# The one-token shift of the first stage: SBUF-to-SBUF DMA and a VectorE subtraction in place of fp32 products

## The chip, the cores and the metric

The kernel runs on one core of a Trainium2 chip. The metric is the time of one execution on the device in microseconds (us); lower is better. A kernel before and a kernel after are compared by the ratio of their medians over repeated runs.

## What is computed

The reference is two transformer-like layers over 256 tokens of width 2048, all in fp32: a block with an RWKV-7 mixer, an mLSTM mixer and a mixture of experts, then two attention layers. The change touches only the start of the RWKV mixer:

```python
u = x @ w_in[i]                                   # (1, 256, IN_COLS)
u_r, u_m, u_g = _split(u, [RWKV_COLS, MLSTM_COLS, GATE_COLS])   # RWKV_COLS = 3360
...
z_prev = jnp.pad(z, ((0, 0), (1, 0), (0, 0)))[:, :-1]
z = z + mu * (z_prev - z)                         # z is u_r
r, k, v, zw, za, zg = _split(z, [1024, 1024, 1024, 64, 64, 160])
```

Each token's row gets `mu` times the difference between the row of the token before and its own. The first token has zeros before it.

## The kernel before

Tokens lie on partitions: token 128 b + p is on partition p, in half b of a tile. So `UR`, the tile of `u_r`, is 128 partitions x 2 halves x 3360 columns, and the token before is on the partition before; only the first token of the second half has its predecessor on partition 127 of the first half.

The products are made with fp32 values split in two float32r halves each (`hi` and `lo`), three products for one. The weight columns come in blocks of 512 (six of them, and a seventh of 288), and a block's weights in eight pieces of 256 rows (512 KB, in the seventh 288 KB). Each piece goes through a chain: SyncE issues its load into one of six buffers as soon as the piece that was there has been halved; ScalarE writes the high half (`split_to` on ScalarE), VectorE the low half (`split_to` on VectorE, L283); TensorE runs 12 matmuls on it. There are three buffers for the halves, so the high half of a piece waits until TensorE has used the piece three before it. Pieces are counted from 0 over the whole kernel; block ci has the pieces 8ci to 8ci + 7. `ahead_of(key)` halves the pieces up to two beyond the one with which `key`'s sum ends, `more(1)` one more, and each engine works its instructions off in the order in which they are written.

For each block `ci` TensorE runs the projection (`proj_a`, L1282), takes a PSUM buffer for `ur.shift` (L1283), waits for `ur.copied` (L1285), which is ScalarE's copy of the block out of PSUM into `UR` (`out_of`, L2713), and multiplies with `shiftd` (ones on the superdiagonal minus the identity) and `carry` (one element that brings partition 127 of the first half into partition 0 of the second), L1286 to L1288. VectorE waits for this sum and for `mub` (mu on all partitions), multiplies it in PSUM and adds it to `UR` (L2251, L2252). Its event `("ur", ci)` is what the RWKV stage waits for. PSUM is a ring of four buffers; a `take` gets the one that was taken longest ago and waits until it was freed. `shiftd` and `carry` are built by Pool (GpSimd) at the start (L2806 to L2810).

Behind the seventh block the RWKV stage begins: TensorE runs three pieces of another projection (`ml.qk`, whose low halves Pool makes), transposes the gates (`rw.lo`, after ScalarE's tanh and sigmoid on the seventh block, L2379 to L2381), then two more pieces and the lora products, which need `loraT`; VectorE multiplies the keys, squares and sums them (L1403 to L1406) before it copies `loraT` (L1411 to L1416).

Of the kernel before, what the change touches and what calls it, by code (L numbers as in the profile page):

```python
# [9 lines left out]
ALU = mybir.AluOpType  # L10
# [328 lines left out]
def build(nc, I, out, plan=None, last=False):  # L339
    with ExitStack() as ctx:  # L340
# [7 lines left out]
        def at(o, n, dt=F32):  # L348
            names[0] += 1
            assert o + n <= TOT, o + n  # L350
            return nc.alloc_sbuf_tensor_at(f"t{names[0]}", [128, n], dt, offset=base + 4 * o)[:, :]

        def alloc(n, dt=F32):
            o = top[0]
            top[0] = o + n + -n % 8
            return at(o, n, dt)

        def tm(c):
            return alloc(2 * c).rearrange("p (b c) -> p b c", b=2)
# [7 lines left out]
        def bufs(nraw, nhalf):  # L367
# [9 lines left out]
        ident, shiftd, carry, ucent, tri_inc, tri_str = [alloc(128) for _ in range(6)]  # L377
# [15 lines left out]
        UR = tm(3360)  # L393
# [4 lines left out]
        PB, QB, RB, BB = tm(1024), tm(1024), tm(1024), tm(1024)  # L398
# [16 lines left out]
        kstate = alloc(8 * 64).rearrange("p (i v) -> p i v", i=8)  # L415
        pz = alloc(8)
        mub = at(fmbase, 3360)
        par = [RB.rearrange("p b c -> p (b c)")[:, 0:1024], RB.rearrange("p b c -> p (b c)")[:, 1024:2048],
               at(lt_at + 1280, 1024)]
        r_, k_, v_ = [UR[:, :, 1024 * i:1024 * i + 1024] for i in range(3)]  # L420
# [142 lines left out]
        def two(v, n):  # L563
            return v.unsqueeze(1).broadcast_to([128, 2, n])

        def half(v):
            return v.rearrange("p (b n) -> p b n", b=2)
# [5 lines left out]
        def tensor_program(e):  # L573
            pe = Tensor(e, counts, ring, stream, ident)
# [71 lines left out]
            def proj_a(*args, **kw):  # L646
                for _ in pieces_a(*args, **kw):
                    pass
# [5 lines left out]
            def some(work, n):  # L654
                for _ in range(n):
                    next(work, None)
# [615 lines left out]
            first = pieces_a(pe, "ur0", xT, 16, "w_in", 0, 512)  # L1272
            for j, part in enumerate(((0,), (0, 1), (1, 2), (2, 3, 3))):
                turn_columns("in.xT", x, j, (f"landed.in{j}",), ("ident",))
                for i in part:
                    pe.wait_ge(("in.xTc", i))
                    some(first, 1)
            pe.wait_ge(("consts",))
            for ci, c in enumerate(range(0, 3360, 512)):
                n = min(512, 3360 - c)  # L1280
                if ci:
                    proj_a(pe, f"ur{ci}", xT, 16, "w_in", c, n)  # L1282
                v = half(pe.take("ur.shift", ci))[:, :, 0:n]  # L1283
                d = UR[:, :, 512 * ci:512 * ci + n]
                pe.wait_ge(("ur.copied", ci))  # L1285
                pe.mm(v[:, 0, :], shiftd, d[:, 0, :], True, True)  # L1286
                pe.mm(v[:, 1, :], shiftd, d[:, 1, :], True, False)
                pe.mm(v[:, 1, :], carry, d[:, 0, :], False, True, event=("ur.shift", ci))  # L1288
            pe.stage("rwkv")
            rwkv()  # L1290
            rows_of("ml.if", "w_if", xT, (0, 8), 8, "pool")
# [10 lines left out]
            v = pe.take("pl.T", of=(2,)).rearrange("p (k b t) -> p k b t", k=4, b=2)  # L1302
# [51 lines left out]
        def vector_program(e):  # L1354
            v = Vector(e, counts, ring, stream)
# [888 lines left out]
                v.split_to(2 * j + 2)  # L2244
            for ci, c in enumerate(range(0, 3360, 512)):
                n = min(512, 3360 - c)
                v.ahead_of("ur.shift", ci)
                ps = half(v.bank("ur.shift", ci))[:, :, 0:n]
                d = UR[:, :, 512 * ci:512 * ci + n]
                v.wait_ge(("ur.shift", ci), ("landed.mu",))  # L2250
                v.tt(ps, ps, two(mub[:, 512 * ci:512 * ci + n], n), ALU.mult)  # L2251
                v.tt(d, d, ps, ALU.add, event=("ur", ci))  # L2252
                v.free("ur.shift", ci)
            v.stage("rwkv")
            rwkv()
            gate_rows()
# [13 lines left out]
            for c in range(4):  # L2270
# [8 lines left out]
                     event=("mi.lo", c))  # L2279
# [46 lines left out]
            first = stream.first("w_in_odd_2")  # L2326
# [16 lines left out]
            for ci in range(4):  # L2343
                cs = slice(512 * ci, 512 * ci + 512)
                for b in range(2):
                    v.stt(hn[:, b, cs], x[:, b, cs], inv[:, b:b + 1], rwt[:, cs], ALU.mult, ALU.mult,
                          event=("out.h", ci) if b else None)


        def scalar_program(e):  # L2350
            a = Scalar(e, counts, ring, stream)
# [16 lines left out]
            def out_of(key, o, ci, f=ACT.Copy, scale=1.0, event=None, tokens=True):  # L2368

                a.ahead_of(key, ci)  # L2370
                ps = a.bank(key, ci)
                a.wait_ge((key, ci))
                ps = half(ps)[:, :, 0:o.shape[2]] if tokens else ps.rearrange("p (m t) -> p m t", m=4)
                a.activation(o, ps, f, scale=scale, event=event)
                a.free(key, ci)
# [335 lines left out]
            for ci, c in enumerate(range(0, 3360, 512)):  # L2711
                n = min(512, 3360 - c)
                out_of(f"ur{ci}", UR[:, :, c:c + n], 0, event=("ur.copied", ci))  # L2713
            a.stage("rwkv")
            rwkv()
            high_halves("rw.yT", yrT, 1024)
# [24 lines left out]
            first = stream.first("w_pg")  # L2741
# [23 lines left out]
            for j in range(4):  # L2765
                ps = a.bank("ev.T", j).rearrange("p (b k t) -> p b k t", b=2, k=4)
                a.wait_ge(("ev.T", j), j > 1 and ("r1.sum", j - 2) or None)
                a.activation(squares[j % 2].rearrange("p (k b t) -> p b k t", k=4, b=2), ps, ACT.Square,
                             event=("r1.square", j))
# [10 lines left out]
            first = stream.first("w_in_odd_2")  # L2780
# [18 lines left out]
        def pool_program(e):  # L2799
            g = Pool(e, counts, ring, stream)  # L2800
# [2 lines left out]
            g.memset(ones, 1.0)  # L2803
            g.memset(ident, 0.0)
            g.asel(ident, ident, ALU.not_equal, 1.0, 0, [[-1, 128]], 1, event=("ident",))
            g.memset(shiftd, 0.0)  # L2806
            g.asel(shiftd, shiftd, ALU.not_equal, 1.0, 1, [[-1, 128]], 1)
            g.asel(shiftd, shiftd, ALU.not_equal, -1.0, 0, [[-1, 128]], 1)
            g.memset(carry, 0.0)
            g.asel(carry, carry, ALU.not_equal, 1.0, -127, [[128, 128]], 1)  # L2810
            g.asel(tri_inc, one, ALU.is_ge, 0.0, 0, [[1, 128]], -1)
            g.asel(tri_str, one, ALU.is_gt, 0.0, 0, [[1, 128]], -1)
            g.memset(ucent, -CD)
# [4 lines left out]
            for l in range(6):  # L2818
                b = 1 << l
# [96 lines left out]
            for l in range(5):  # L2916
                n = 1 << l
# [6 lines left out]
            for l in range(3):  # L2924
                n = 1 << l
# [87 lines left out]
        with nc.Block() as block:  # L3013
            @block.sync
            def _(e):
                sync_program(e)

            @block.tensor
            def _(e):
                tensor_program(e)  # L3020

            @block.vector
            def _(e):
                vector_program(e)

            @block.scalar
            def _(e):
                scalar_program(e)

            @block.gpsimd  # L3030
            def _(e):
                pool_program(e)
# [55 lines left out]
```

## Time and profile before

| | us |
|---|---|
| median of three runs | 3218.98 |
| lowest and highest run | 3209.98, 3226.59 |
| span of the profiled execution | 3213.3 |
| TensorE busy in it | 3035.3 (94%) |
| VectorE, ScalarE, Pool busy in it | 1550.1, 837.7, 266.6 |
| the first stage in it, to the last shift product | 0 to about 190 |

The profile is one execution. PE is TensorE's matmuls, PEld its weight loads, DVE VectorE, ACT ScalarE, POOL GpSimd, SP SyncE; nearly every instruction is recorded in a helper of the program (L137 the matmul, L143 the transpose, L254 ScalarE's activation, L283 VectorE's two-operand operation), so shapes and moments tell them apart. L83 and L2970 are DMA issues. The time behind "<-" in brackets is for how long the engine had been idle, and what ended it. A granted clock (PEclk) of 1.00 is 2.4 GHz, 0.50 is 1.2 GHz.

### The profile page before, as it was taken

How to read it: one execution, taken by the hardware profiler on the slowest of the kernel's cores; microseconds unless marked ns; L12 is line 12 of the kernel's file. 1: busy time of each engine (PE TensorE's matmuls, PEld its weight loads, DVE VectorE, ACT ScalarE, POOL GpSimd, SP SyncE). 2: the span in 40 equal slices, each digit the busy share in tenths (PEclk: the TensorE clock that was granted, in tenths of full speed). 3: DMA queues.
4: the chain of work that ended last, by engine and by line, in shares of the span. 5: the costliest groups of instructions: out<-in, count | busy, mean ns of one | idle time of the engine just before them, and what ended most of it. 6: DMA issues, size and time to landing. Idle time of an engine off the chain costs nothing.

```text
span 3213.3 us, 42675 instructions
## 1 busy us (share of the span) xinstructions
PE 3035.3 (94%) x18308; PEld 2171.3 (68%) x18308; DVE 1550.1 (48%) x1862; ACT 837.7 (26%) x926; POOL 266.6 (8%) x245
## 2 busy tenths in 40 slices
PE   8999999899999999999999999799999999999998
PEld 6787777899987733333333333288768878997886
DVE  4465544674555513222222322438886554444655
ACT  3342222544433311011101100110001334443443
POOL 2042111000000000000000000054330000000000
PEclk9999988999998999999999999899999999999899
DMA  7543221456564599999999999743333465887443
GB/s 243 152 136 99 74 67 55 119 161 180 177 228 152 211 413 425 425 425 425 425 425 425 425 425 425 291 140 118 117 119 118 144 175 122 184 189 158 99 158 138
DMA packets 215216, 722.10 MB, mean 225 GB/s; under 512 B 16170, under 2 KB 18634, under 8 KB 164716
## 3 DMA queue, kind: packets, MB, share of 16 engines
q1 hardware_dynamic: 210716, 702.22, 62.6%
q0 software_dynamic: 3216, 14.97, 1.3%
q8 instruction: 146, 2.39, 0.3%
q10 hardware_dynamic: 1088, 2.10, 0.2%
q14 instruction: 50, 0.41, 0.0%
HBM read 717.13 MB, written 2.10 MB: 224 GB/s over the span
## 4 chain that ended last, share of the span: by engine, by line
PE 73%; DMA 12%; DVE 10%; ACT 4%; issue 1%; POOL 0%; DVEq 0%; ACTq 0%
PE psum L137 72%; DMA t<-in_w_up 11%; DVE t L283 7%; ACT t L254 2%; PE psum L143 1%; DVE t L294 1%; ACT t L256 1%; DVE t L298 0%; DVE t L306 0%; ACT L254 0%; POOL t L328 0%; DVE t L269 0%; ACT L256 0%; DMA t<-in_x 0%; DVE t L275 0%
## 5 line engine op out<-in xcount | busy, mean ns | idle before, releaser
L137 PE MATMUL psum<-t,t 128*128 128x256 f32 (+10 forms) x17230 | 2941.4, 380 | 125.5 <-DVE t L283 69.3
L137 PEld LDWEIGHTS psum<-t,t 128*128 128x128 f32 (+4 forms) x17230 | 2080.0, 175 | 948.1 <-issue 580.3
L283 DVE TENSOR_TENSOR t<-t,t 128x1024 fp32r<-128x1024 f32 (+6 forms) x642 | 785.0, 1223 | 502.1 <-ACT t L254 469.1
L254 ACT ACTIVATE t<-t 128x1024 fp32r<-128x1024 f32 (+8 forms) x521 | 528.5, 1014 | 924.5 <-PE psum L137 661.2
L283 DVE TENSOR_TENSOR t<-t,psum 128x1024 f32<-128x1024 f32 (+3 forms) x265 | 246.4, 930 | 739.5 <-PE psum L137 439.0
L254 ACT ACTIVATE t<-psum 128x1024 f32<-128x1024 f32 (+5 forms) x278 | 213.5, 768 | 1408.7 <-PE psum L137 1310.4
L328 POOL TENSOR_TENSOR t<-t,t 128x1024 f32<-128x1024 f32 (+9 forms) x125 | 209.0, 1672 | 545.4 <-DVE t L283 258.2
L283 DVE TENSOR_TENSOR t<-psum,t 128x1024 f32<-128x1024 f32 (+5 forms) x125 | 100.2, 802 | 131.6 <-PE psum L137 103.0
L143 PE MATMUL psum<-t,t 128*128 128x128 f32 (+1 forms) x566 | 87.7, 294 | 32.1 <-DVE t L294 18.4
L143 PEld LDWEIGHTS psum<-t,t 128*128 128x128 f32 (+1 forms) x566 | 67.3, 149 | 69.6 <-issue 39.8
L83 POOL DMA_DIRECT2D t<-in_s_lr x1 | 0.6, 574 | 1185.1 <-DVE t L306 1185.1
L269 DVE COPY t<-psum 128x256 f32<-128x256 f32 (+4 forms) x82 | 47.7, 582 | 105.8 <-PE psum L143 59.6
L294 DVE SCALAR_TENSOR_TENSOR t<-t,t,t 128x512 f32<-128x512 f32 (+4 forms) x80 | 49.4, 618 | 3.0
L254 ACT ACT_TABLE_LOAD x38 | 48.8, 1283 | 4.6 <-issue 1.4
L298 DVE TENSOR_REDUCE t<-t 128x4 f32<-128x512 f32 (+9 forms) x58 | 47.5, 819 | 3.5 <-ACT t L254 1.4
L302 DVE TENSOR_TENSOR_SCAN t<-t,t 128x256 f32<-128x256 f32 (+1 forms) x65 | 44.7, 688 | 2.2
L290 DVE TENSOR_SCALAR t<-t,t,t 128x64 f32<-128x64 f32 x128 | 40.2, 314 | 4.6
L137 PE MATMUL psum<-t 64*64 64x64 f32 (+2 forms) x512 | 36.2, 267 | 6.5 <-ACT t L254 5.8
L83 POOL DMA_DIRECT2D t<-in_final_norm_g x1 | 0.6, 567 | 483.4 <-PE psum L137 483.4
L137 PEld LDWEIGHTS psum<-t 64*64 64x64 f32 (+2 forms) x512 | 30.0, 172 | 10.0 <-ACT t L254 7.5
L269 DVE COPY t<-t 64x64 f32<-64x64 f32 x64 | 30.2, 472 | 2.2
L256 ACT ACTIVATE t<-psum,t 128x256 f32<-128x256 f32 (+1 forms) x56 | 24.9, 444 | 21.5 <-PE psum L137 15.1
(65 smaller groups left out, 237.9 us busy)
## 6 DMA issues: line engine op xcount, KB each, us to landing
t<-in_w_gate SPq DMA_DIRECT2D x128, 1024.0 KB, 16.9
t<-in_w_up SPq DMA_DIRECT2D x128, 1024.0 KB, 18.4
t<-in_w_down SPq DMA_DIRECT2D x128, 1024.0 KB, 17.4
t<-in_w_in SPq DMA_DIRECT2D x160, 512.0 KB, 4.3
t<-in_w_in_odd SPq DMA_DIRECT2D x128, 512.0 KB, 5.3
t<-in_w_in_even SPq DMA_DIRECT2D x96, 512.0 KB, 3.8
t<-in_w_out SPq DMA_DIRECT2D x32, 512.0 KB, 4.7
t<-in_w_pg SPq DMA_DIRECT2D x32, 512.0 KB, 4.1
```

What stands on the lines that cost most here:

```text
L83: self.e.dma_start(out, in_).then_inc(self.counts.sem(name), 16)
L137: ins = self.e.matmul(o, l, r, start=start, stop=stop, skip_group_check=True)
L143: ins = self.e.transpose(o, i, self.ident[0:k, 0:k])
L254: self.put(self.e.activation(o, i, f, scale=scale), event)
L256: self.put(self.e.activation(o, i, f, bias=bias, scale=scale), event)
L269: self.put(self.e.tensor_copy(o, i), event)
L283: self.put(self.e.tensor_tensor(o, a, b, op), event)
L290: self.put(self.e.tensor_scalar(o, a, s1, s2, o1, o2), event)
L294: self.put(self.e.scalar_tensor_tensor(out=o, in0=a, scalar=s, in1=b, op0=o1, op1=o2), event)
L298: self.put(self.e.tensor_reduce(o, i, AX.X, op), event)
L302: self.put(self.e.tensor_tensor_scan(o, d0, d1, init, o0, o1), event)
L328: self.put(self.e.tensor_tensor(o, a, b, op), event)
```

## The change

The products with `shiftd` and `carry` go, with their constants and their PSUM buffers. ScalarE, after it has copied a block into `UR`, waits for its own copy and, from block 2 on, for VectorE's addition of two blocks before, and issues two DMAs from its own queue: partitions 0 to 126 of the block to partitions 1 to 127 of `prior`, and the row of partition 127, first half, to partition 0, second half. `prior` is double-buffered, in the region of `QB`, which is used only later. Partition 0 of the first half is zeroed once by Pool. VectorE waits for both DMAs, subtracts (`prior` - `UR`) into `gap` (the region of `BB`), multiplies by mu and adds. Ahead of the wait it halves the pieces up to 8ci + 10 (`split_to(8 * ci + 11)` ends before piece 8ci + 11), and one more between the subtraction and the multiplication.

```diff
@@ names @@
+        prior = [QB.rearrange("p b c -> p (b c)")[:, 1024 * k:1024 * k + 1024].rearrange("p (b c) -> p b c", b=2)
+                 for k in range(2)]
+        gap = BB[:, :, 0:512]
@@ tensor_program @@
-            pe.wait_ge(("consts",))
             for ci, c in enumerate(range(0, 3360, 512)):
                 n = min(512, 3360 - c)
                 if ci:
                     proj_a(pe, f"ur{ci}", xT, 16, "w_in", c, n)
-                v = half(pe.take("ur.shift", ci))[:, :, 0:n]
-                d = UR[:, :, 512 * ci:512 * ci + n]
-                pe.wait_ge(("ur.copied", ci))
-                pe.mm(v[:, 0, :], shiftd, d[:, 0, :], True, True)
-                pe.mm(v[:, 1, :], shiftd, d[:, 1, :], True, False)
-                pe.mm(v[:, 1, :], carry, d[:, 0, :], False, True, event=("ur.shift", ci))
@@ vector_program @@
-                v.ahead_of("ur.shift", ci)
-                ps = half(v.bank("ur.shift", ci))[:, :, 0:n]
+                v.split_to(8 * ci + 11)
+                p_ = prior[ci % 2][:, :, 0:n]
                 d = UR[:, :, 512 * ci:512 * ci + n]
-                v.wait_ge(("ur.shift", ci), ("landed.mu",))
-                v.tt(ps, ps, two(mub[:, 512 * ci:512 * ci + n], n), ALU.mult)
-                v.tt(d, d, ps, ALU.add, event=("ur", ci))
-                v.free("ur.shift", ci)
+                v.wait_ge(("landed.prior", ci), ("landed.mu",))
+                v.tt(gap[:, :, 0:n], p_, d, ALU.subtract)
+                v.more(1)
+                v.tt(gap[:, :, 0:n], gap[:, :, 0:n], two(mub[:, 512 * ci:512 * ci + n], n), ALU.mult)
+                v.tt(d, d, gap[:, :, 0:n], ALU.add, event=("ur", ci))
@@ scalar_program @@
                 out_of(f"ur{ci}", UR[:, :, c:c + n], 0, event=("ur.copied", ci))
+                a.wait_ge(("ur.copied", ci), ("first.row",), ci > 1 and ("ur", ci - 2) or None)
+                p_ = prior[ci % 2][:, :, 0:n]
+                a.load(("landed.prior", ci), [(p_[1:128], UR[0:127, :, c:c + n]), (p_[0:1, 1:2], UR[127:128, 0:1, c:c + n])])
@@ pool_program @@
-            g.memset(shiftd, 0.0)
-            g.asel(shiftd, shiftd, ALU.not_equal, 1.0, 1, [[-1, 128]], 1)
-            g.asel(shiftd, shiftd, ALU.not_equal, -1.0, 0, [[-1, 128]], 1)
-            g.memset(carry, 0.0)
-            g.asel(carry, carry, ALU.not_equal, 1.0, -127, [[128, 128]], 1)
+            for k in range(2):
+                g.memset(prior[k][0:1, 0, :], 0.0, event=("first.row",))
```

## Rows read from the trace of the kernel before

**Rows 1.** Page, busy time, share of the span and instructions by engine.
```profile
PE 3035.3 (94%) x18308; PEld 2171.3 (68%) x18308; DVE 1550.1 (48%) x1862; ACT 837.7 (26%) x926; POOL 266.6 (8%) x245
```

**Rows 2.** Busy time in stretches: stretch, length, engines, clock, DMA share; shift 2 to 3.
```profile
66.19:92.46 26.27, 25.16 (x102) 19.15 (x102) 12.26 (x10) 9.50 (x9) 0.00 (x0) 1.00 0.55 160
```

**Rows 3.** Timeline of 65 to 80 us: start, duration, engine, operation; a full boundary.
```profile
65.12 1.02 ACT L254 ACTIVATE t<-psum 128x1024 f32<-128x1024 f32 x1 [1.70 <-PE psum L137]
...
66.19 14.00 PE L137 MATMUL psum<-t,t 128*128 128x512 f32 x54 [1.11 <-ACT t L254]
...
69.07 1.23 DVE L283 TENSOR_TENSOR psum<-psum,t 128x1024 f32<-128x1024 f32 x1 [4.40 <-PE psum L137]
70.34 1.22 DVE L283 TENSOR_TENSOR t<-t,psum 128x1024 f32<-128x1024 f32 x1
...
71.92 1.06 ACT L254 ACTIVATE t<-t 128x1024 fp32r<-128x1024 f32 x1 [4.63 <-PE psum L137]
...
77.49 1.06 ACT L254 ACTIVATE t<-t 128x1024 fp32r<-128x1024 f32 x1 [1.73 <-PE psum L137]
```

**Rows 4.** Chain of waits from 118 to 206 us: start, duration, what.
```profile
170.25 1.03 ACT t L254
...
171.33 2.86 PE psum L137 x6
...
177.62 9.88 PE psum L137 x72
...
187.52 0.66 ACT t L254
...
196.88 0.31 ACT t L254
...
199.03 1.06 PE psum L143 x8
200.09 6.13 PE psum L137 x49
```

**Rows 5.** DMA between 3204 and 3214 us, ScalarE's stores: packets, queue, issues.
```profile
DMA packets 1088, 2.10 MB, mean 210 GB/s; under 512 B 64, under 2 KB 64, under 8 KB 1088
...
q10 hardware_dynamic: 1088, 2.10, 54.0%
...
out<-t ACTq DMA_DIRECT2D x4, 512.0 KB, 2.7
```

**Rows 6.** DMA between 194 and 195.6 us, the load of the 65 rows of `w_w2`.
```profile
DMA packets 78, 0.27 MB, mean 166 GB/s; under 512 B 13, under 2 KB 13, under 8 KB 78
```

**Rows 7.** PE's wait in the timeline of 231 to 237 us, and clock by stretches.
```profile
236.03 1.23 PE L137 MATMUL psum<-t,t 128*128 128x256 f32 x8 [2.78 <-POOL t L328]
...
236.00:240.00 4.00, 3.98 (x23) 3.98 (x24) 3.93 (x3) 0.00 (x0) 3.86 (x1) 0.66 0.48 131
240.00:244.00 4.00, 4.00 (x36) 4.00 (x35) 3.97 (x2) 0.00 (x0) 2.70 (x2) 0.91 0.50 135
244.00:248.00 4.00, 4.00 (x23) 4.00 (x23) 3.93 (x3) 1.23 (x2) 2.42 (x1) 0.57 0.41 131
```

**Rows 8.** DMA between 162 and 166 us, loads of 1152-byte packets.
```profile
DMA packets 354, 0.39 MB, mean 97 GB/s; under 512 B 16, under 2 KB 354, under 8 KB 354
...
q1 hardware_dynamic: 354, 0.39, 40.8%
```

**Rows 9.** Timeline behind the last block and, last, at 231 us.
```profile
190.78 0.75 DVE L283 TENSOR_TENSOR t<-t,psum 128x576 f32<-128x576 f32 x1
...
191.64 3.54 DVE L283 TENSOR_TENSOR t<-t,t 128x2048 f32<-128x2048 f32 x1
...
195.21 4.37 DVE L283 TENSOR_TENSOR t<-t 128x2048 f32<-128x2048 f32 x1
...
203.95 0.48 DVE L279 MEMSET t<- 1x512 f32 x1 [0.16 <-DVE t L269]
...
231.37 2.29 DVE L283 TENSOR_TENSOR t<-t 128x2048 f32<-128x2048 f32 x1
```

**Rows 10.** DMA issues up to 240 us: size, median time to landing.
```profile
t<-in_w_in SPq DMA_DIRECT2D x64, 512.0 KB, 4.5
```

## What will the change do to the time?

> **What bounds the kernel now.** I read the page first: PE is busy 94% of a span of 3213.3 us [rows 1], so what PE waits for or works off counts directly. The change touches the first stage only, so I went on to the busy time by stretches, one stretch for each column block. The reader should see that a full block takes 26.3 us, of which PE is busy 25.2, while VectorE (12.3) and ScalarE (9.5) are half idle [rows 2]. The timeline of one boundary shows what the missing 1.1 us and part of the busy time are [rows 3]. I call T the moment when the last projection product of a block ends. ScalarE copies the block out of PSUM (65.12 to 66.14), PE waits 1.11 us for that, then does the shift (66.19 to 69.05, three fp32 products that appear as six matmuls), and VectorE multiplies by mu and adds (1.23 + 1.22 us). After this ScalarE's halvings of the next pieces start 2.79 us apart (71.92 to 77.49 for two): this is the time of one piece, 12 matmuls, and eight pieces are 22.4 us. So the shift costs PE 26.3 - 22.4 = 3.9 us for each full block. The chain of waits has the last two: 4 us from 170.23 to 174.19, then 0.7 us of waiting after 187.49 and six matmuls of 0.28, until VectorE multiplies at 189.98 and adds at 190.78 [rows 4, 9]. Between T = 170.23 and T = 187.49 lie 17.3 us, with the narrow block's eight pieces of 1.6 us (72 matmuls, six pieces, in 9.88).
>
> **What is removed and moved.** PE loses the wait and the products: six times 3.9 us, and 2.4 in the last block, at most 26 us. Not all of it is to be had. The PSUM ring takes the buffer used longest ago; without the shift's own buffers, block 1 falls on block 0's, so that boundary keeps the 1.2 us wait for the copy: 2.7 instead of 3.9. Pool's five constant builders go and two one-partition memsets come: Pool's instructions are done before the first T in any case, nothing. VectorE's two operations become three. The subtraction I price as the fp32 operation of the same size, 1.23 us (0.76 in the narrow block) [rows 3]. With the gaps: 1.27 a step.
>
> **What the new wait holds back.** VectorE now waits for the landing before it subtracts, and it is a queue in order: behind the wait stand the low halves of the next weight pieces, without which PE has nothing. Written out: before the wait VectorE has halved pieces up to the third of the next block (8ci+10); the fourth (8ci+11) comes after the subtraction, the fifth (8ci+12) only after mu and the addition. With L for the landing, counted from T: the fourth is ready at L + 2.6, the fifth at L + 6.4. PE wants the fifth at T + 4 x 2.8 = 11.2. So the landing is free up to L = 4.7, and each us above it costs a us at every full boundary. VectorE gets to the wait at about T + 4.5, because ScalarE now issues two DMAs ahead of the third piece's high half. There is no slack to speak of. The weight loads, too, are issued on SyncE as pieces are halved, and stand still with VectorE.
>
> **How long the transfer takes.** This decides the case. It is 127 partitions with 2 runs of 2048 bytes each, 254 packets. The nearest row in direction and queue is ScalarE's store at the end: 512 KB on 128 partitions, 2.7 us from issue to landing; its four stores left 1088 packets, 64 of them tiny, so 16 tiny ones (the completion of each DMA engine) for a DMA. The share of 54.0% of 16 engines over 10 us is 86.4 us, 84 ns for each of 1024 packets of 2 KB [rows 5]. On 16 engines the data are 16 x 84 ns = 1.34 us and the rest, 1.36 us, is fixed.
>
> But does a DMA of 127 partitions get 16 engines? The trace has one load whose partitions are not a multiple of 16, `w_w2` with 65 rows of 4 KB. In its stretch there are 78 packets, 13 of them tiny [rows 6]: 65 data packets and 13 completions, so 13 engines with 5 rows each, where 16 engines with uneven shares would have left 16. The hardware gave equal shares. That admits two rules: the largest number up to 16 that divides the count (65 = 13 x 5), or shares of the count over 16 rounded up (5, which just fills 13). For 127, a prime, the first gives one engine, the second 16. I take the first, because equal shares is what the row shows and for 127 only one engine gives them.
>
> The Trainium skill, page DMA: Bandwidth & Descriptors, section Why a DMA increments its semaphore by 16 and not by 1, says that a DMA from the SP or ACT queue uses the largest k up to 16 that divides the slowest dimension, and names 127 partitions as k = 1; the rounded-up shares it knows for the software queue. By that rule the transfer is the serial one, by the rounded-up rule the transfer of rival one; this trace's 13 completions for 65 rows agree with it and do not exclude the other.
>
> One engine: 254 x 84 ns = 21.3 us. The bounds are 1.34 us (16 engines) and twice 21.3 (if an engine that reads and writes SBUF takes twice the time of one that only does one of them; no row has that). I take 21.3, since loads and stores have the same packet time. Beside it the weight loads go through the same engine with 16 packets each, 1.34 us; two of them fall into the wait (the pieces whose halving frees a buffer just before T and at T + 4.5), then they stop with VectorE: 2.7 us, between 0 and 5.4. So L = 1.1 (copy and semaphore) + 1.36 + 21.3 + 2.7 = 26.5.
>
> **The sum.** A full boundary, blocks 0 to 4: 26.5 to the landing, 6.4 until the fifth piece can start, four more pieces 4 x 2.8 = 11.2, together 44.1. PE has then stood still for some 20 us. In this trace a wait of PE of 2.78 us, at 233.25 to 236.03, is followed by stretches with a granted clock of 0.66, 0.91 and 0.57, that is 2.7 + 0.7 + 3.4 = 6.9 us at the lower level of 1.2 GHz, 3.4 us of PE's work [rows 7]. Here the first us of such a loss fall into VectorE's time; I take 1.0 for a boundary, between 0 and 3.4. So 45.1 against 26.3: +18.8, five times: +94.
> Block 5's shift beside the narrow block: its loads are 288 KB, so L is 25.4; two steps of 1.27, the subtraction too, and two low halves of 0.8 make the fifth piece ready 5.4 later; four pieces of 1.6 are 6.4; clock 0.8. 38.0 against 17.3: +20.7.
> The last block: 254 packets of 1152 bytes. The narrow loads' row gives 40.8% of 16 engines over 4 us for 338 data packets, 77 ns, waits for HBM in it [rows 8]; by bytes it is 84 x 1152/2048 = 47. I take 51, nearer to the latter since the source is SBUF: 13.0 us. Landing at T + 0.75 + 1.36 + 13.0 + 4 (three loads of ml.qk) = 19.1, three steps of 0.8: the block is ready at T + 21.5, where it was ready at 191.53, T + 4.0 [rows 9]. Behind it VectorE's chain for the key norm runs 12.8 us (191.64 to 204.43 [rows 9]) to the lora inputs; 3.3 of them were Pool's doing (3.54 and 4.37 us where an operation of that size took 2.29 with Pool idle [rows 9]), and Pool will be idle. PE needs the gates (tanh at 196.88, transposes at 199.03: 2.2 later, so at T + 23.7), then the transposes and two pieces (1.1 and 6.0 us, and 1.5 for the clock) and the lora inputs (T + 31.0): the first lora product at T + 32, against 206.1, T + 18.6 [rows 4]: +13.4.
> Sum: 94 + 20.7 + 13.4 = +128 us. The later stages wait for this one's results and move with it; the stage of the experts is bound by loads that start only when the mixer is done. The profiled execution spans 3213.3 us, 5.7 under the median of 3219.0; on the median it gives 3347 us. The bounds together (no contention, no clock: -19 and -6; double contention and full clock loss: +19 and +16; packet time 10% up or down: +-14; an issue on ScalarE that lasts until the engine has taken the descriptors: +9) make 3295 to 3425 for this case.
>
> **Rival one, faster: the transfer is spread over 16 engines.** L is then 1.1 + 2.7 = 3.8 with nothing beside it, and 1.1 + 4.5 = 5.6 at the weight loads' median [rows 10]. Below 4.7 no stall: 4 x 3.9 + 2.7, and 0.6 for block 5 (there the three steps on VectorE eat the rest, as PE wants a piece every 1.6 us), nothing at the end: -19, 3200 us. At 5.6: 0.9 lost at six boundaries, 3205 us. For it: the row of 65 rows bears the rounded-up shares as well. It would turn into a loss from L = 8.
>
> **Rival two, much slower: one engine at half the rate between SBUF and SBUF.** 21.3 more at six boundaries and 13 at the last: +141 on the forecast, 3488 us. Against it: nothing in the trace shows an engine below 84 ns for 2 KB unless HBM kept it waiting.
>
> **How the numbers follow.** One engine at the packet time of the trace: 0.80, at 3347 us. Rival one 0.12, rival two 0.08; the range leaves these out, 2 in 10, and is that of the likeliest case. A measurement of this kernel can tell 0.5%, 16 us. The first rival lies on that bound, 14 to 19 us faster: 0.07 faster, 0.05 within. Slower: 0.88.
>
> **What the profile after would show.** For the forecast: on ScalarE's queue 254 data packets and one completion for a transfer, a landing some 25 us after the issue; VectorE idle on that DMA seven times, some 20 us each; PE standing after the third piece of each block, for VectorE; 45 us from block to block; a low granted clock just after. If ScalarE's DMA instruction itself lasts for 20 us, PE stands a piece earlier. Against it: 16 completions for a transfer and landings under 6 us. It would be wrong in size if packets in SBUF took another time than 84 ns.

## The result, and the profile after

| | before | after |
|---|---|---|
| median, us | 3215.69 (4 runs) | 3351.84 (4 runs) |
| ratio, 95% interval | | 1.0419 (1.0398 to 1.0440) |
| span of the profiled execution | 3213.3 | 3352.8 |

The kernel after is 4.2% slower, 136 us on the medians, against a forecast of 3347 us. The first rows are the chain of waits of the kernel after, 30 to 360 us (share by line, then start, duration, what), around one block boundary, then the last block. They answer to [rows 4].

```profile
by line: DMA t<-t 49.4%; PE psum L137 37.6%; DVE t L283 6.6%; ACT t L254 3.3%; ACTq L83 1.7%; PE psum L143 0.6%; issue 0.6%; ACT L254 0.4%; DVEq L77 0.1%; ACTq L77 0.0%
...
84.53 1.03 ACT t L254
85.59 0.75 ACTq L83
86.37 24.50 DMA t<-t
110.90 1.24 DVE t L283
112.26 1.24 DVE t L283
113.54 16.04 PE psum L137 x60
129.60 1.04 ACT t L254
...
304.51 0.66 ACT t L254
305.19 0.73 ACTq L83
305.96 16.76 DMA t<-t
322.74 2.76 DVE t L283
325.52 0.77 DVE t L283
326.32 0.77 DVE t L283
```

The reader should see one repeated pattern: copy (84.53), DMA of 24.5 us, two steps of VectorE (the subtraction and the low half of the fourth piece), then the last five pieces of the block on TensorE (60 matmuls), and the next copy at 129.60. T, the end of the block's last projection product, is 84.51, just before the copy; the landing (VectorE's start at 110.90) is 26.4 later, the period from copy to copy 45.07 us. In the kernel before the DMA has no place in that chain.

What the engines do in that time, from the timeline of 84 to 118 us, answers to [rows 3].

```profile
85.59 13.30 ACTq L83 DMA_DIRECT2D t<-t  x2
98.94 3.40 ACT L254 ACTIVATE t<-t 128x1024 fp32r<-128x1024 f32 x3 [13.38 <-issue]
...
101.31 5.49 PE L137 MATMUL psum<-t,t 128*128 128x512 f32 x12 [11.21 <-DVE t L283]
...
110.90 7.82 DVE L283 TENSOR_TENSOR t<-t,t 128x1024 f32<-128x1024 f32 x6 [9.64 <-DMA t<-t]
...
113.54 4.83 PE L137 MATMUL psum<-t,t 128*128 128x512 f32 x12 [6.74 <-DVE t L283]
```

TensorE stands 11.2 us, does one piece, stands another 6.7, and the pieces after a wait take 5.49 and 4.83 us where a piece in stride takes 2.8. The busy time by stretches tells why (the number behind the busy times of the five engines is the granted clock, 1.00, 0.50 and 0.50 here, which answers to [rows 7]):

```profile
88.00:92.00 4.00, 2.09 (x9) 1.33 (x8) 0.00 (x0) 0.00 (x0) 0.00 (x0) 1.00 0.07 21
...
96.00:100.00 4.00, 0.00 (x0) 0.00 (x0) 0.00 (x0) 1.06 (x1) 0.00 (x0) 0.50 0.07 26
100.00:104.00 4.00, 2.69 (x6) 2.16 (x7) 1.23 (x1) 2.11 (x2) 0.00 (x0) 0.50 0.43 137
```

And the transfer itself, from the DMA view of 85.5 to 111 us, which answers to [rows 5] and [rows 6]:

```profile
q10 hardware_dynamic: 287, 0.52, 5.7%
```

287 packets for a pair of DMAs on ScalarE's queue. 254 are the data of 127 partitions. The row of partition 127 is cut in 16 parts and has 16 completions, so 32. That leaves one: one completion, one engine. 5.7% of 16 engines over 25.5 us is 23.3 us for 254 packets, at most 92 ns each (at most, because the tiny packets' time is in it). From 90 to 102 us no packet of a weight load ran beside it, and the transfer alone left

```profile
DMA packets 175, 0.30 MB, mean 25 GB/s; under 512 B 30, under 2 KB 30, under 8 KB 175
```

that is 145 data packets in 12 us, 83 ns for each, where the prediction had 84.

### The profile page after: what moved, and what is told of

It reads as the page before. It is cut to its first block, busy times and chain, and to the rows that moved or that the text cites. A ratio compares the mean times of both kernels' runs of the same rounds, so it can differ in the third digit from the quotient of the medians.

```text
span 3352.8 us, 42608 instructions
## 1 busy us (share of the span) xinstructions
PE 3053.7 (91%) x18266; PEld 2189.8 (65%) x18266; DVE 1556.4 (46%) x1869; ACT 837.9 (25%) x926; POOL 261.9 (8%) x242
## 4 chain that ended last, share of the span: by engine, by line
PE 70%; DMA 16%; DVE 9%; ACT 3%; issue 1%; ACTq 0%; POOL 0%; DVEq 0%
PE psum L137 68%; DMA t<-in_w_up 11%; DVE t L283 7%; DMA t<-t 5%; ACT t L254 2%; PE psum L143 1%; DVE t L294 1%; ACT t L256 1%; DVE t L306 0%; ACT L254 0%; POOL t L328 0%; DVE t L269 0%; DVE t L298 0%; ACTq L83 0%; ACT L256 0%
## 5 line engine op out<-in xcount | busy, mean ns | idle before, releaser
L137 PE MATMUL psum<-t,t 128*128 128x256 f32 (+11 forms) x17188 | 2960.3, 382 | 243.6 <-DVE t L283 183.5
L137 PEld LDWEIGHTS psum<-t,t 128*128 128x128 f32 (+5 forms) x17188 | 2098.9, 177 | 1065.5 <-issue 571.8
L283 DVE TENSOR_TENSOR t<-t,t 128x1024 fp32r<-128x1024 f32 (+6 forms) x663 | 809.1, 1220 | 660.1 <-ACT t L254 555.5
L283 DVE TENSOR_TENSOR t<-t,psum 128x1024 f32<-128x1024 f32 (+3 forms) x258 | 238.3, 924 | 744.2 <-PE psum L137 443.7
L137 PEld LDWEIGHTS psum<-t 64*64 64x64 f32 (+2 forms) x512 | 29.8, 172 | 10.1 <-ACT t L254 7.5
## 6 DMA issues: line engine op xcount, KB each, us to landing
t<-in_w_up SPq DMA_DIRECT2D x128, 1024.0 KB, 18.9
```

The source lines that it names most:

```text
L137: ins = self.e.matmul(o, l, r, start=start, stop=stop, skip_group_check=True)
L283: self.put(self.e.tensor_tensor(o, a, b, op), event)
```

## The experiments

Each is compared with the kernel before on the same chip: the first four with a median before of 3217.57 us, the next two with 3220.62, the last two with 3217.45. The first four change how the transfer of the kernel after is issued and nothing else. T0 to T5 are the copies of the first to the sixth block; where the text says so, times are from one traced execution and not from the medians.

**The transfer over all engines.**

```diff
-                a.load(("landed.prior", ci), [(p_[1:128], UR[0:127, :, c:c + n]), (p_[0:1, 1:2], UR[127:128, 0:1, c:c + n])])
+                a.load(("landed.prior", ci), [(p_[1:113], UR[0:112, :, c:c + n]), (p_[113:128], UR[112:127, :, c:c + n]), (p_[0:1, 1:2], UR[127:128, 0:1, c:c + n])])
```

> The transfer of 127 partitions is cut in two, 112 and 15 partitions; nothing else differs from the kernel after. Theory one (the number of DMA engines that a partition count gets sets the landing, and the landing sets the stage): 16 and 15 completions for the two, 14 and 2 packets of 2 KB for each engine, landing 4.3 to 5.6 us after the block's last product instead of 26.5, no wait of 20 us on VectorE, TensorE never idle for more than 2 us in the stage; 3196 to 3205 us against 3216 of the kernel before, 14 to 20 us faster. Rival theory (the copy between partitions is slow by itself, or the third VectorE operation and its place in the queue cost the time): landings still above 15 us or block periods still above 40 us, and 3330 us or more.

3218.09 us against 3217.57, ratio 0.9997 (0.9985 to 1.0009): the whole loss of 4.2% goes, and nothing is gained. The mechanism is theory one's, its time is not: 14 to 20 us faster was expected. The chain of 36 to 205 us (first line) and the timeline of 63 to 95 us show the landing and what it holds:

```profile
66.51 3.57 DMA t<-t
...
63.81 1.02 ACT L254 ACTIVATE t<-psum 128x1024 f32<-128x1024 f32 x1 [1.69 <-PE psum L137]
64.86 2.56 ACTq L83 DMA_DIRECT2D t<-t  x3
67.47 3.41 ACT L254 ACTIVATE t<-t 128x1024 fp32r<-128x1024 f32 x3 [2.63 <-issue]
68.56 1.23 DVE L283 TENSOR_TENSOR t<-t,t 128x1024 fp32r<-128x1024 f32 x1 [5.18 <-ACT t L254]
...
70.10 9.18 DVE L283 TENSOR_TENSOR t<-t,t 128x1024 f32<-128x1024 f32 x7 [0.31 <-DMA t<-t]
...
76.62 17.00 PE L137 MATMUL psum<-t,t 128*128 128x512 f32 x72 [0.83 <-DVE t L283]
```

The landing is at T + 6.3 (63.79 to 70.10; at other boundaries where the trace shows it 6.6 and 7.2), since the three issues take 2.6 to 3.1 us on ScalarE in the full blocks and the last DMA, though only 2 KB, lands last: it is issued by 66.5 and lands 3.6 us later. The prediction's free limit was 4.7. This block takes 24.3 us (63.81, 88.07) instead of 26.3, and 22.4 would have been TensorE's own time.

**Two engines, and four.** The same edit with 122 and 5 partitions, and with 124 and 3.

> Cut in 122 and 5 partitions. By the divisor rule 122 = 2 x 61 runs on 2 engines, 5 on 5. Theory one, with the terms of the prediction: 122 packets of 84 ns on an engine are 10.2 us, landing at 1.1 + 1.4 + 10.2 + 1.3 = 14.0; a full block 14.0 + 6.4 + 11.2 + 0.5 for the clock = 32.1 against 26.3, five times +29; block 5 +9; the end +5: 3259 us. If the shares were rounded up over 16 engines the time would be that of the cut in 112 and 15. If each engine beyond one gave nothing (the source or target is the limit, not the engine): 3340 us.

> Cut in 124 and 3 partitions: 124 = 4 x 31 on 4 engines. Theory one: 62 packets on an engine are 5.2 us, landing at 1.1 + 1.4 + 5.2 + 0.7 = 8.4, near the point of no gain and no loss that the prediction put at 8: 3.7 above what VectorE's queue hides, 3.9 saved on TensorE. 3210 to 3222 us, that is the same as before. If the landing were hidden further than 4.7 us: below 3205. If the stall grew faster than the landing: above 3230.

Two engines: 3279.77 us, ratio 1.0199 (1.0183 to 1.0215). Four engines: 3261.76, ratio 1.0136 (1.0117 to 1.0156). Both are slower than expected, 3259 and the same as before. The packets of a boundary, from the DMA view of the kernel on four (71 to 83 us) and of the one on two (110 to 126 us):

```profile
q10 hardware_dynamic: 293, 0.52, 15.1%
```

```profile
q10 hardware_dynamic: 293, 0.52, 9.7%
```

Data and the row's 32 leave 7 completions in both, 4 + 3 and 2 + 5. (The cut in 112 and 15 left 317 packets, so 31 completions, 16 + 15.) Shares rounded up over 16 engines would have left 16 + 5 for the cut at 122, where the largest divisor up to 16 is 2. So the divisor decides, here on three counts of partitions for the large transfer. What missed is the time. On four engines the landing came at T + 12.2 instead of 8.4, on two at T + 16.3 instead of 14.0. By the shares above a packet took at most 29.0 us / 254 = 114 ns on four engines and 98 on two, where 84 had been assumed. The weight loads beside it are not what makes four engines slower: from 75 to 78 us of the kernel on four engines no load's packet ran, and the view has only

```profile
DMA packets 119, 0.20 MB, mean 65 GB/s; under 512 B 24, under 2 KB 24, under 8 KB 119
...
q10 hardware_dynamic: 119, 0.20, 25.1%
```

95 data packets in four engines' 12 us, so 101 to 127 ns for one, by how much of the time the 24 tiny ones are given, against 83 for one engine alone. Why is open. It is a part of the miss only: 62 packets at 30 ns more are 1.9 of the 3.8 us. The rest (the loads' share, the last DMA's late issue) no run takes apart. The time on four engines is above the 3230 us set for a stall that grows faster than the landing; the table below shows that it does not, the landing came later. Behind the last block the two kernels lose 7.8 and 6.5 us more.

The kernels together test the sum of the prediction for a full boundary, period = L + 6.4 + 11.2 and a rest, in which the prediction put the clock. One boundary of each trace:

| data engines | L, us | L + 17.6 | period, us | rest |
|---|---|---|---|---|
| 1 (after) | 26.4 | 44.0 | 45.1 | 1.1 |
| 2 | 16.3 | 33.9 | 35.0 | 1.1 |
| 4 | 12.2 | 29.8 | 30.6 | 0.8 |
| 16 and 15 | 6.3 | 23.9 | 24.3 | 0.4 |

Four landings, one line: from 6.3 to 26.4 us of landing, each us of landing is a us of the block. Over all five full boundaries the rest is 0.7 to 2.1, 0.7 to 1.8, 0.6 to 0.8 and, where the trace shows the landing, 0.35. It shrinks with TensorE's standing time and as the mean granted clock of these blocks rises: 0.77, 0.85, 0.94, 1.00. What is left at a clock of 1.00, 0.35 us, is not the clock.

**The row's DMA first.** The small DMA is issued ahead of the large one.

> The small DMA (the row of partition 127) is issued ahead of the large one, still on one engine; the rest is the kernel after. In the kernel after ScalarE stood 11 to 15 us at the issue of the two. Theory a (the second DMA's issue is held until the one engine has taken most of the first's descriptors): the stand goes, ScalarE makes the high halves at once, TensorE runs a third piece before it stands; but the landing is the same, so the time stays within 5 us of 3352. Theory b (the large one's own issue lasts as long as its descriptors need room): the stand stays at 11 to 15 us, and so does the time. Rival in time (the stand of ScalarE is part of the loss): 3320 or less.

3358.80 us, ratio 1.0440 (1.0424 to 1.0457), where the kernel after has 1.0419. The landing came at T + 27.1 in the boundary shown; in the first six it is 0.3 to 0.8 us later than in the kernel after. In the last block it is 4.7 us later (22.9 against 18.2): ScalarE went on, and 2.36 MB of loads ran beside it where it had been 1.32. The time is 7 us more, 2 beyond what theory a had. On the issues theory a holds: in the timeline of 85 to 116 us

```profile
86.86 1.35 ACTq L83 DMA_DIRECT2D t<-t  x2
88.26 2.24 ACT L254 ACTIVATE t<-t 128x1024 fp32r<-128x1024 f32 x2 [1.43 <-issue]
...
115.57 0.80 PE L137 MATMUL psum<-t,t 128*128 128x512 f32 x1 [21.43 <-DVE t L283]
```

both issues take 1.35 us instead of 13.30, and ScalarE goes on. So it was the small DMA's issue that stood, and only because it came behind the large one. TensorE now stands once, 21.4 us, where it stood 11.2 and 6.7. The time is no better: period less landing is 18.9 us here and 19.0 in the kernel after (means of five), so ScalarE's stand had cost some 0.1 us a boundary, and the later landing took more than that.

**More pieces ahead of the wait.** With the cut in 112 and 15, VectorE's order is changed (called the spaced kernel below):

```diff
-                v.split_to(8 * ci + 11)
+                v.split_to(8 * ci + 12)
...
                 v.tt(gap[:, :, 0:n], gap[:, :, 0:n], two(mub[:, 512 * ci:512 * ci + n], n), ALU.mult)
+                v.more(1)
                 v.tt(d, d, gap[:, :, 0:n], ALU.add, event=("ur", ci))
```

> The cut in 112 and 15, and on VectorE one more low half before the wait for the landing and one more between the multiplication and the addition, so the wait stands behind four pieces of the next block. Theory one: the landing is then free up to 7 us instead of 4.7 and no low half comes late; TensorE goes through the full blocks with 22.4 to 22.6 us each but for the first (1.2 more for the PSUM buffer), 3194 to 3200 us. If the landing of the cut in 112 and 15 was below 4.7 us already, it is equal to that kernel within 3 us.

3210.27 us against 3220.62, ratio 0.9962 (0.9949 to 0.9975): faster, by half of what was expected (3194 to 3200). The copies come at 63.21, 86.38, 109.91, 133.28: 23.2 to 23.5 us apart, not 22.4 to 22.6. The chain of 36 to 215 us says what is left:

```profile
86.38 1.04 ACT t L254
87.44 0.67 ACTq L83
88.14 0.91 ACTq L83
89.08 1.31 ACTq L83
90.44 1.07 ACT t L254
91.53 1.24 DVE t L283
92.81 17.07 PE psum L137 x72
```

The landing is gone from it. ScalarE's three issues (0.67, 0.91, 1.31) stand ahead of the high half that TensorE wants next; the last experiment tests this. The last block costs 5.5 us more than before, which the expectation had left out.

**The wait alone.** The kernel before, with the first piece of the next block ahead of the shift (the kernel with the later shift):

```diff
+            sums = [None] + [pieces_a(pe, f"ur{ci}", xT, 16, "w_in", c, min(512, 3360 - c))
+                             for ci, c in enumerate(range(0, 3360, 512)) if ci]
...
                 if ci:
-                    proj_a(pe, f"ur{ci}", xT, 16, "w_in", c, n)
+                    some(sums[ci], 8)
+                if ci < 6:
+                    some(sums[ci + 1], 1)
                 v = half(pe.take("ur.shift", ci))[:, :, 0:n]
```

> The kernel before with its fp32 products, but TensorE runs the first piece of the next block ahead of the shift, so that it doesn't wait for ScalarE's copy. It gives the wait's part of the cost by itself: six boundaries of 3.9 us are 1.1 of wait and 2.8 of products. Theory: 5 x 1.1 + at most 1.1 at the first boundary, where the PSUM ring gives the buffer still to be copied: 5 to 7 us faster than before, 3210 us. If the products alone are the cost and the wait is hidden: 3216.

3216.56 us against 3220.62, ratio 0.9983 (0.9974 to 0.9992). On the medians that is 4.1 us, where 5 to 7 were expected. In the traces it takes 126.2 us from T0 to T5 (38.17 to 164.34) and the kernel before 131.6: 5.4, as worked out, nothing at the first boundary and 1.3 at each of the next four. So of the 3.9 us that the shift costs at a boundary, 1.1 to 1.3 are the wait and can be had without any DMA.

**The last block with products.** As the spaced kernel, but the seventh block keeps `ur.shift` with its products and VectorE's two operations on PSUM; ScalarE issues no DMA for it.

```diff
+            pe.wait_ge(("consts",))
+            v = half(pe.take("ur.shift", 6))[:, :, 0:288]
+            d = UR[:, :, 3072:3360]
+            pe.wait_ge(("ur.copied", 6))
+            pe.mm(v[:, 0, :], shiftd, d[:, 0, :], True, True)
...
```

> As the kernel with the cut in 112 and 15 and the low halves spaced, but the last block (288 columns) keeps the fp32 products and the multiplication in PSUM of the kernel before; Pool builds their constants again. It tells what the last block's DMA costs. Theory: from the end of the last block's products to ScalarE's first copy of a lora result the kernel before takes 20.0 us and the spaced one 25.5, of which the landing is 7 us instead of 2.5 for the products, and VectorE's operations between SBUF operands take 2.7 us instead of 0.8 while Pool works. With the products back this stretch is 20.0 again: 5 to 6 us faster than the spaced kernel, about 3205 us where before is 3220. If the stretch is set by TensorE and Pool and not by the shift: no difference.

3206.61 us against 3217.45, ratio 0.9965 (0.9953 to 0.9977). From the last block's copy to the first lora copy it takes 20.15 us (171.92 to 192.07), where the spaced kernel took 25.5 (172.53 to 198.03) and before 20.0. The traces show the 5 us in this stretch. The 5 to 6 us less in all that were expected are not shown: the ratios of the two kernels, 0.9962 and 0.9965, don't tell them apart.

**The high half ahead of the issues.** In addition, on ScalarE:

```diff
+                a.more(1)
                 a.wait_ge(("ur.copied", ci), ("first.row",), ci > 1 and ("ur", ci - 2) or None)
```

> In addition ScalarE makes the high half of the third piece of the next block before it issues the DMAs. Theory: in the spaced kernel the three issues (2.7 to 3.7 us) stand ahead of that high half, and TensorE loses 0.8 to 1.1 us at each boundary, period 23.2 to 23.5 instead of 22.4. The landing gets 1.1 us later, to some 7.4 after the block's end, just inside what the spaced order hides (7). So a period of 22.4 to 22.8, 3 to 5 us less in all: about 3201 us where before is 3220. If the landing is too late then, TensorE stands before the fifth piece instead, and the gain is gone.

3198.84 us against 3217.45, ratio 0.9942 (0.9927 to 0.9958), 0.6% faster than before. 3201 was expected. This is the lowest median of the study; its interval overlaps a little with that of the kernel with products in the last block. Its chain of 36 to 195 us and its busy time from 60 to 160 us, some four blocks:

```profile
40.30 112.14 PE psum L137 x480
...
60.00:160.00 100.00, 99.10 (x446) 80.93 (x444) 55.74 (x47) 42.48 (x43) 0.00 (x0) 1.00 0.69 199
```

TensorE is busy 99.1 of 100 us at a granted clock of 1.00; the blocks are 22.3 to 22.4 us apart (63.09, 85.49, 107.84, 130.15). In these full blocks the shift costs TensorE nothing, and the loss of the spaced kernel at the issues is gone. What is left is 1.5 us at the first boundary, in it the wait for the PSUM buffer, and the shift beside the narrow block: there the landing is 7.6 us after the block's end (160.02), TensorE waits 2.6 us, and the block takes 18.2 us, where the kernel with the later shift takes 15.9.

Not all that a trace gains in this stage is found in the medians. At the first lora copy the traces have the kernel cut in 112 and 15, the spaced one, the one with the later shift and the last two 2.3, 9.5, 7.3, 15.5 and 16.8 us ahead of the kernel before; the medians have them 0.5 behind and 10.4, 4.1, 10.8 and 18.6 ahead. A difference of some 5 us between two of these kernels is not settled by their times.

## Why the prediction was right, point by point

**One engine for 127 partitions: right, and shown.** It was the choice between two readings of the 13 completions of [rows 6]. The count of completions in the kernel after is one, and the cuts at 122 and 124 give two and four. The Trainium skill, page DMA: Bandwidth & Descriptors, section Why a DMA increments its semaphore by 16 and not by 1, gives this rule; the traces agree with it.

**The landing at T + 26.5: right.** Measured 25.7 to 26.7 at the six boundaries with a transfer of 508 KB, 26.3 in the mean of the first five. Its terms nearly hold: the queue's packets took 23.3 us at most, where 21.3 + 2.7 had been put down, and what is left between issue and landing (85.59 to 110.90) is 2.0 us instead of 1.36; the two errors of 0.7 us cancel. That loads and stores have the same packet time was taken without a row: over 66 to 92 us of the kernel before, the weight loads' packets took at most 111 ns in the mean.

**A full boundary at 45.1 us: right.** From the first copy to the sixth it is 226.9 us, 45.4 each; the sum had +94, the traces give +95.3. The clock's 1.0 was the least sure of the terms; the rest is 1.1 in the table and 1.4 in the mean of the five. The way it comes about is as worked out: at the boundary shown the fourth piece, 4.83 us at the lower clock instead of 2.8, ends at 118.37, about 1.1 us after VectorE has the fifth ready (110.90 + 6.4), so that 2 us of loss cost 1.1.

**Block 5 and the end.** +20.7 forecast, 39.1 us against 17.3 measured, +21.8; the landing was 1.0 later than the forecast's 25.4. For the end +13.4 forecast; from the last copy to the first lora copy 34.8 us (304.51 to 339.35) against 20.0, +14.8. The 1.4 more have a cause that the sum did not have: the subtraction took 2.76 us, not 0.76, beside Pool (the last section), of which a landing 0.85 sooner than forecast took some back. That Pool would be idle held only for the key norm behind it (2.29 us at 329.51). The three together: 128 forecast, 131.9 in the two traces. The remaining 7.7 us between the spans lie behind the stage. There the profiled execution of before was quicker than that of the kernel with the later shift too, which was 7.3 us ahead at the first load of `w_g` and 0.1 at the first load of `w_br`; so at least a part of them belongs to that execution and not to the change. Between medians the difference is 136.

**The range.** The bounds named in the prediction, added up, give 3308 to 3405 us; the range of 3295 to 3425 is wider by 13 and 20 us for which it gives no term. The measured time lies well inside both.

**What the prediction had as possible and was so.** ScalarE's DMA instruction lasted 13 us and TensorE stood a piece earlier. The price of +9 that stood with it in the bounds was too high: the kernel with the row first shows some 0.1 us a boundary.

**Rival one had the right point of decision and the wrong time.** A us for a us above a free limit is what the table shows, and its line, carried on to 22.4 us, meets the forecast's limit of 4.7 within the rest; no kernel had a landing below it. But its 14 to 19 us of gain did not come, and two terms were at fault. The issues: the landing was bounded by 3.8 and 5.6 from single DMAs, while three issues on ScalarE last 2.6 to 3.1 us and the last one lands last: 6.3. And the end: it had nothing at the last block, and there the kernel cut in 112 and 15 loses 6.4 us (178.77 to 205.20, against 20.0). The chain from the landing over VectorE's three steps (186.03 to 192.04, so 13.3 us after the block's end, against 4.0 before) to the gates sets that stretch, as in the forecast's own sum; TensorE waits 5.9 us for it. Of the 8.9 us won by T5 (161.28 against 170.25), 2.3 are left at the first lora copy. Its break-even at a landing of 8 was wrong for the same reason, the end: the kernel cut in 112 and 15 is even at 6.3. Rival two fell with the packet time, 83 ns on one engine alone.

## What to carry to other kernels

Before a DMA replaces products, look at its partition count: on every count seen here (127, 124, 122, 112, 65, 15) the number of engines was the largest divisor up to 16, and a shift by one partition makes it 127, a prime. Cut such a transfer so that each part divides well (112 and 15), and count the completions in the trace to be sure. Then look at what is queued in order behind the wait and behind the issues: here the same idea came out 4.2% slower, even, or 0.6% faster, by the cut, by the halvings moved ahead of the wait and ahead of the issues, and by leaving the last block, whose result is wanted at once, to TensorE.

## What the runs showed of the hardware that was not expected

**A DMA's issue can stand behind an earlier one on few engines.** In the first six blocks the row's DMA held ScalarE until 13 to 15 us after the first issue when it came behind 254 packets on one engine, and the two issues took 1.3 to 2.0 us when it came first. It goes by the number of engines: the three issues of a full block took 4.9 to 5.2 us with two engines, 3.2 to 3.5 with four and 2.6 to 3.1 with 16 and 15. What inside the queue holds the issue was not tried.

**VectorE slows between SBUF operands beside Pool.** These are lines of the spaced kernel's timeline of 172 to 198 us, then of its chain. The subtraction and the multiplication of the last block run beside Pool's low halves:

```profile
179.14 2.39 POOL L328 TENSOR_TENSOR t<-t,t 128x1024 fp32r<-128x1024 f32 x1 [0.17 <-POOL t L328]
...
181.70 2.64 POOL L328 TENSOR_TENSOR t<-t,t 128x1024 fp32r<-128x1024 f32 x1 [0.17 <-POOL t L328]
```

```profile
179.47 2.69 DVE t L283
182.18 2.79 DVE t L283
184.99 0.77 DVE t L283
```

2.69 and 2.79 us beside Pool, 0.77 after it, for the same shape. That it is Pool and not the operation shows in the kernel with the row first, where Pool was idle at this point (its last low half began at 317.03) and the subtraction of the last block, here in its chain of 300 to 350 us, took

```profile
331.63 0.77 DVE t L283
```

In the lines above VectorE ran beside Pool for 2.1 and 2.2 us and took 1.9 and 2.0 us longer than 0.77: by this estimate it hardly moved while Pool's operation ran. The operations with an operand in PSUM that the kernel before had in this place took 0.77 and 0.75, though Pool was at work then, too; from its timeline of 187 to 207 us, beside [rows 9]:

```profile
188.09 2.38 POOL L328 TENSOR_TENSOR t<-t,t 128x1024 fp32r<-128x1024 f32 x1 [0.17 <-POOL t L328]
...
189.98 0.77 DVE L283 TENSOR_TENSOR psum<-psum,t 128x576 f32<-128x576 f32 x1 [5.73 <-PE psum L137]
190.63 2.40 POOL L328 TENSOR_TENSOR t<-t,t 128x1024 fp32r<-128x1024 f32 x1 [0.17 <-POOL t L328]
```

So taking a step out of PSUM can cost more than the step. By what the two hinder each other, no run here shows.

**A packet between SBUF partitions took longer on four engines and more than on one.** For 2 KB, by the shares of the queue: at most 92 ns with one engine, 98 with two, 114 with four and 125 with 16 and 15 (28.4% of 16 engines over 64 to 71 us, 254 packets), with weight loads beside them. Without loads it was 83 on one engine and 101 to 127 on four, so the loads are not the reason; 84 for the stores at the end, on 16 engines [rows 5]. The cause is open.
